# Quad attention of a hybrid encoder: sums by a column of ones, copies on ScalarE, spread loads and weight splits at the end of a turn

## The chip, the core and the metric

One core of a Trainium2 chip runs the whole program. The metric is the device time of the program in microseconds. Engines: TensorE (PE, with its weight loads PEld), VectorE (DVE), ScalarE (ACT), GpSimd (POOL) and SyncE (SP), which here only issues DMAs.

## What is computed

Two sequences of 256 and 512 tokens with 2048 features (768 tokens, six tiles of 128) go through two layers. Each layer is

```python
h = rms_norm(x, ln_g[l]).astype(x.dtype)
proj = jnp.einsum('bsd,de->bse', h, w_in[l])        # q, k, v, gate of mixers A, B, C
ya = window_sink_attention(...)                      # +-128 tokens, bias, sink
yb = global_axial_attention(...)                     # dense, rotary
yc = dilated_mixture_attention(...)                  # three groups of (window, dilation)
mix = concat([ya * silu(ga), yb * silu(gb), yc * silu(gc)])
x = x + jnp.einsum('bse,ed->bsd', mix, w_out[l])
```

The change is in mixer C. It has 8 heads in 2 key groups of 4 heads, each for the patterns `(128, 1), (512, 4), (2048, 16)`. For each pattern

```python
s = jnp.einsum('bqhrd,bqkhd->bhrqk', qblk[:, :, g], kg) + biases[g]
s = jnp.where(valid[None, None, None], s, NEG_INF)
lse = jax.nn.logsumexp(s, axis=-1)
p = jnp.exp(s - lse[..., None])
outs.append(jnp.einsum('bhrqk,bqkhd->bqhrd', p, vg))
```

and the three results of a head are summed with the softmax of their `lse` as weights. All is float32.

## The kernel before

A layer has three phases. First the input projection: PE multiplies normed features by slabs of weights, each as a high and a low part; SP loads the weights, ScalarE rounds the high part (`split_hi`, L1818), DVE subtracts to get the low part (`split_lo`, L2099). Heads are normed, turned and stored to DRAM (`heads_t`, `keys_t`, `v_rows`). Then the attention loop of `N_LOOP` turns, with one step for each turn, while PE also works off pieces of the gate projection (`gate_piece`, L1644 to L1646). Last the output projection. In layer 0 the loop begins at 651 us, in layer 1 at 2028 us.

Steps come in units (`ATT_UNITS`), the quads first. A quad unit takes four heads of mixer C with a dilated pattern; there are four of them, of six steps each (one for each tile of tokens): units 0 and 2 are open (dilation 4), units 1 and 3 packed (dilation 16, where the tokens of a tile fall in four classes of 32, and the four heads of a class share one 128x128 block of scores). So turns 0 to 5 and 12 to 17 score open steps, 6 to 11 and 18 to 23 packed ones. Units of mixer A follow from turn 24. An item is what one query tile is loaded for; in quads items and steps are the same.

In turn i of the quads the engines do, in this order:
- PE: scores of step i (L1674 and L1675 open, L1669 packed); gate pieces; transposes of the probabilities of step i-3 (`p_turn`, L1694); product with the values of step i-4 (`pv`, L1734 open, L1715 packed). Scores have two banks, so those of step i wait until step i-2 is `biased`.
- ScalarE: take the packed product of step i-5 (`take_packed`, L1928), weight splits due (`SPLIT_AT`: turns 0, 9, 15, 22, 25), copy of the turned probabilities of step i-3 if the step is odd (`copy_pt`, L1154), exponentials of step i (`exp_step`: open, L1901, four with `accum_out` for the sums; packed, L1894, one).
- DVE: weight splits due, take the open product of step i-5 (`take_part`, L2293), bias and minima of step i (L2225 open; L2179 to L2186 packed), for packed steps the sums of step i-3 (`packed_sums`, L2192), copy of even steps i-3.
- SP, a queue in order, for item `it`: `load_item(it)` (L1309) once step it-4 is scored; then the stores, key, value, bias and part loads that the tables (`PARTS_AT`, `KEYS_AT`, `VALUES_IN_AT`, `BIASES_AT`, ...) put at that item; then gate weights. `load_bias` (L1297) issues four transfers for a quad unit, `load_blocks` (L1273) eight: they place the values of each class in the diagonal blocks of `blocks0` and `blocks1`, which POOL zeroes before (L2597). Before the loop SP loads biases, keys and values of the first two units and stores the last value slab (`store_values`, L1199).

Results of a quad step, with minima and sums, go into a slot of `part_out` and to DRAM (`store_part`, L1378), and come back in `load_parts` when mixer C merges the three patterns in eight merges.

## Time and profile before

| | us |
|---|---|
| median of 3 runs (2768.97 to 2772.97) | 2769.77 |
| the profiled execution | 2773.48 |
| its span, first to last instruction | 2771.7 |
| PE busy | 2728.9 |
| DVE busy | 1614.7 |
| ScalarE busy | 1190.9 |
| POOL busy | 943.0 |
| quad turns of layer 0 (651.06 to 709.08) | 58.02 |
| quad turns of layer 1 (2028.38 to 2083.23) | 54.85 |

Times in the profile count from the first instruction. A busy time is the sum of an engine's instructions without overlap; those of PE are pipelined, so "busy" is not "at its peak". Matmuls at half clock are also busy. "Idle before, releaser" at the end of a row is the time for which an engine did nothing before that instruction, and what let it go on. SPq is SP's queue of DMA issues: the time there is that of the issue, not of the transfer.

### The profile page before, as it was taken

How to read it: one execution, taken by the hardware profiler on the slowest of the kernel's cores; microseconds unless marked ns; L12 is line 12 of the kernel's file. 1: busy time of each engine (PE TensorE's matmuls, PEld its weight loads, DVE VectorE, ACT ScalarE, POOL GpSimd, SP SyncE). 2: the span in 40 equal slices, each digit the busy share in tenths (PEclk: the TensorE clock that was granted, in tenths of full speed). 3: DMA queues.
4: the chain of work that ended last, by engine and by line, in shares of the span. 5: the costliest groups of instructions: out<-in, count | busy, mean ns of one | idle time of the engine just before them, and what ended most of it. 6: DMA issues, size and time to landing. Idle time of an engine off the chain costs nothing. (4 is left out here: it accounts for less than half of the span.)

```text
span 2771.7 us, 43372 instructions
## 1 busy us (share of the span) xinstructions
PE 2728.9 (98%) x14505; PEld 2444.1 (88%) x14505; DVE 1614.7 (58%) x3901; ACT 1190.9 (43%) x2897; POOL 943.0 (34%) x864
## 2 busy tenths in 40 slices
PE   8999999999999999999999999999999999999999
PEld 7888899988999999988888888999889999998887
DVE  3345644434676677667743466444356766766776
ACT  4322222224565566544542222222256655664443
POOL 0333333320465377600003334333205743774000
PEclk9999999999999999999999999999999999999999
DMA  5366556658544443464524565666685345325535
GB/s 175 105 185 199 181 184 189 180 171 229 149 134 125 118 116 87 145 245 124 202 92 119 187 194 179 193 175 178 184 232 147 115 118 155 94 70 210 198 122 182
DMA packets 439415, 442.53 MB, mean 160 GB/s; under 512 B 103863, under 2 KB 333399, under 8 KB 439196
## 3 DMA queue, kind: packets, MB, share of 16 engines
q1 hardware_dynamic: 439196, 439.77, 53.0%
q8 instruction: 118, 1.93, 0.3%
q14 instruction: 101, 0.83, 0.1%
HBM read 313.91 MB, written 125.75 MB: 159 GB/s over the span
## 5 line engine op out<-in xcount | busy, mean ns | idle before, releaser
L1818 ACT CAST w_hi<-w_raw 128x512 fp32r<-128x512 f32 x640 | 397.2, 622 | 695.2 <-PE bank L1590 430.3
L1588 PE MATMUL bank<-w_hi,act_hi 128*128 128x512 f32 x1728 | 689.1, 399 | 0.0
L2099 DVE TENSOR_TENSOR w_lo<-w_raw,w_hi 128x512 fp32r<-128x512 f32 x640 | 457.8, 716 | 391.9 <-ACT w_hi L1818 389.0
L1590 PE MATMUL bank<-w_hi,act_lo 128*128 128x512 f32 x1728 | 679.0, 393 | 0.0
L1589 PE MATMUL bank<-w_lo,act_hi 128*128 128x512 f32 x1728 | 677.6, 392 | 0.0
L2548 POOL TENSOR_SCALAR prob<-prob,denom 128x256 f32<-128x256 f32 (+2 forms) x288 | 348.8, 1216 | 243.1 <-DVE denom L2263 239.8
L1590 PEld LDWEIGHTS bank<-w_hi,act_lo 128*128 128x128 f32 x1728 | 372.6, 216 | 54.0
L1588 PEld LDWEIGHTS bank<-w_hi,act_hi 128*128 128x128 f32 x1728 | 373.3, 216 | 50.0
L1589 PEld LDWEIGHTS bank<-w_lo,act_hi 128*128 128x128 f32 x1728 | 373.3, 216 | 48.8
L1644 PE MATMUL bank<-act_hi,w_hi 128*128 128x384 f32 x1024 | 348.8, 341 | 0.0
L1646 PE MATMUL bank<-act_hi,w_lo 128*128 128x384 f32 x1024 | 345.9, 338 | 0.0
L1645 PE MATMUL bank<-act_lo,w_hi 128*128 128x384 f32 x1024 | 345.6, 338 | 0.0
L1621 PE MATMUL bank<-w_hi,a_part 128*128 128x512 f32 x672 | 263.2, 392 | 5.7 <-DVE a_part L2391 3.0
L2254 DVE TENSOR_TENSOR pt_lo<-bank,pt_hi 128x256 fp32r<-128x256 f32 (+2 forms) x288 | 154.2, 535 | 188.3 <-ACT pt_hi L1920 186.2
L1622 PE MATMUL bank<-w_lo,a_part 128*128 128x512 f32 x672 | 261.7, 389 | 0.0
L1623 PE MATMUL bank<-w_hi,a_part 128*128 128x512 f32 x672 | 261.6, 389 | 0.0
L2539 POOL TENSOR_TENSOR y<-y,gains 128x256 f32<-128x256 f32 (+1 forms) x144 | 159.8, 1122 | 265.7 <-DVE y L2132 265.7
L2165 DVE TENSOR_TENSOR turned<-bank,turned 128x512 fp32r<-128x512 f32 (+2 forms) x120 | 64.8, 557 | 278.3 <-ACT turned L1885 278.2
L1885 ACT CAST turned<-bank 128x512 fp32r<-128x512 f32 (+2 forms) x120 | 55.3, 482 | 365.0 <-PE bank L1566 355.9
L1694 PE MATMUL bank<-ident,prob 128*128 128x128 f32 x1128 | 195.7, 274 | 5.7 <-POOL prob L2548 5.7
L1645 PEld LDWEIGHTS bank<-act_lo,w_hi 128*128 128x128 f32 x1024 | 193.9, 189 | 4.2
L1914 ACT ACTIVATE prob<-prob,minus_max 128x257 f32<-128x257 f32 (+2 forms) x240 | 128.2, 534 | 161.2 <-DVE minus_max L2245 160.4
(135 smaller groups left out, 4500.7 us busy)
## 6 DMA issues: line engine op xcount, KB each, us to landing
w_raw<-w_in SPq DMA_DIRECT2D x144, 512.0 KB, 4.8
w_sums<-sum_out SPq DMA_DIRECT2D x32, 1280.0 KB, 6.8
w_raw<-w_sums SPq DMA_DIRECT2D x80, 512.0 KB, 4.1
sum_in<-w_out SPq DMA_DIRECT2D x64, 512.0 KB, 5.6
heads_t<-turned SPq DMA_DIRECT2D x240, 128.0 KB, 2.4
q_t<-heads_t SPq DMA_DIRECT2D x192, 128.0 KB, 2.1
k_t<-keys_t SPq DMA_DIRECT2D x48, 384.0 KB, 5.8
w_raw<-w_out SPq DMA_DIRECT2D x32, 512.0 KB, 3.7
```

The lines of the kernel that those rows point to most:

```text
L1588: pe.matmul(acc[t][:], hi, w_hi[:, W_AT[n]:W_AT[n] + SLAB], start=(k == 0), stop=False)
L1589: pe.matmul(acc[t][:], hi, w_lo[:, W_AT[n]:W_AT[n] + SLAB], start=False, stop=False)
L1590: last = pe.matmul(acc[t][:], lo, w_hi[:, W_AT[n]:W_AT[n] + SLAB], start=False, stop=(k == KC - 1))
L1621: pe.matmul(bank[at][:], hi[:, tokens], w_hi[:, W_AT[n]:W_AT[n] + SLAB], start=(j == 0), stop=False)
L1622: pe.matmul(bank[at][:], hi[:, tokens], w_lo[:, W_AT[n]:W_AT[n] + SLAB], start=False, stop=False)
L1623: last = pe.matmul(bank[at][:], lo[:, tokens], w_hi[:, W_AT[n]:W_AT[n] + SLAB], start=False, stop=(j == KH - 1))
L1644: pe.matmul(out, hi, act_hi[:, k, tokens], start=(k == 0), stop=False)
L1645: pe.matmul(out, hi, act_lo[:, k, tokens], start=False, stop=False)
L1646: last = pe.matmul(out, lo, act_hi[:, k, tokens], start=False, stop=(k == KC - 1))
L1818: nc.scalar.copy(w_hi[:, W_AT[n]:W_AT[n] + SLAB], w_raw[:, load % W_RAW, j, :]).then_inc(w_hi_done, 1)
L2099: nc.vector.tensor_tensor(w_lo[:, W_AT[n]:W_AT[n] + SLAB], w_raw[:, load % W_RAW, j, :], w_hi[:, W_AT[n]:W_AT[n] + SLAB].bitcast(F32), ALU ...
L2548: nc.gpsimd.tensor_scalar(v, v, denom[:, pair % STAT_SLOTS, st["r"]:st["r"] + 1], None, ALU.mult)\
```

## The change

- Values get a 65th column of ones: `v_t` and `blocks` are 65 wide, POOL sets the ones, and the quad products write 4 x 65 columns, so that the sum of the probabilities comes out of the product. The exponentials of open steps lose `accum_out`, and `packed_sums` goes, with the waits on it.
- `part_out`, `part_rows` and `part_in` hold, for each head, 64 values, sum and minimum (`ROW` = 66). `load_parts` loses one small transfer.
- `on_act`: ScalarE copies the turned probabilities of all packed steps, and of odd open ones as before.
- `load_blocks` is issued in four pairs, one for each class at successive items (4 to 7 for unit 1, 20 to 23 for unit 3), in place of eight at once (before the loop, and at item 21).
- Biases of quad units 2 and 3 are loaded head by head, at items 11 to 14 and 17 to 20, in place of all four at items 10 and 16.
- Before the loop the last value slab is stored ahead of the loads of keys and biases of unit 1.
- In quad turns other than 0, `split_hi` comes behind the exponentials and `split_lo` behind the copy.

```diff
--- before.py
+++ after.py
@@ -410,7 +409,7 @@
-    return step % 2 == 1
+    return step % 2 == 1 or packed(STEPS[step]["unit"])
...
@@ -630,9 +629,12 @@
 KEYS_AT = at_items((u, UNIT_LAST[u - KV_SLOTS] + 1) for u in range(KV_SLOTS, len(ATT_UNITS)))
-VALUES_IN_AT = at_items((u, UNIT_LAST[u - KV_SLOTS] + PAIR_LAG + 1) for u in range(KV_SLOTS, len(ATT_UNITS)))
+VALUES_IN_AT = at_items((u, UNIT_LAST[u - KV_SLOTS] + PAIR_LAG + 1) for u in range(KV_SLOTS, len(ATT_UNITS)) if not packed(ATT_UNITS[u]))
+BLOCKS_AT = at_items(((u, c), (UNIT_LAST[u - KV_SLOTS] + PAIR_LAG if u >= KV_SLOTS else 0) + c)
+                     for u, x in enumerate(ATT_UNITS) if packed(x) for c in range(CLASSES))
 MERGE_IN_AT = at_items((mc, end - 2 * TT + 1 + PAIR_LAG + 1 if mc == 0 else MERGE_END[mc - 1] + OWN_TURN + 2) for mc, end in enumerate(MERGE_END))
-BIASES_AT = at_items((b, BIAS_LAST[b - 2] + 1) for b in range(2, len(BIAS_SETS)))
+BIASES_AT = at_items(((b, heads), BIAS_LAST[b - 2] + 1 + (1 + heads[0] if BIAS_SETS[b][1] is None else 0))
+                     for b in range(2, len(BIAS_SETS)) for heads in (((0,), (1,), (2,), (3,)) if BIAS_SETS[b][1] is None else ((0, 1),)))
...
@@ -711,7 +713,9 @@
         top[0] -= 4 * TT * 2 * DH
-        blocks1 = sb("blocks1", [P, TT // 2, CLASSES, DH])
+        blocks1 = sb("blocks1", [P, TT // 2, CLASSES, DH + 1])
+        top[0] -= 4 * (TT // 2) * CLASSES * (DH + 1)
+        top[0] += 4 * TT * 2 * DH
...
@@ -1261,18 +1255,18 @@
-            def load_blocks(l, u):
+            def load_blocks(l, u, c):
                 unit = ATT_UNITS[u]
-                sp.wait_ge(blocks_zeroed, 2 * (l + 1))
+                sp.wait_ge(ones_set, 2 * CLASSES * (l + 1))
                 if u >= KV_SLOTS:
...
                 rows = v_rows[:, unit["v"] * DH:(unit["v"] + 1) * DH].rearrange("(h t m c) n -> h c m t n", h=2, t=TT // 2, c=CLASSES)
-                for half, c in itertools.product(range(2), range(CLASSES)):
-                    sp.dma_start(blocks[half][c * PACK:(c + 1) * PACK, :, c, :], rows[half, c]).then_inc(blocks_loaded, 16)
-
-            def load_bias(l, b):
+                for half in range(2):
+                    sp.dma_start(blocks[half][c * PACK:(c + 1) * PACK, :, c, 0:DH], rows[half, c]).then_inc(blocks_loaded, 16)
+
+            def load_bias(l, b, heads=range(4)):
...
@@ -1280,7 +1274,7 @@
                 w = TABLE_COLS[kind]
-                for h in range(4 if hp is None else 2):
+                for h in heads if hp is None else range(2):
...
@@ -1320,13 +1314,12 @@
                 j, hp = first["unit"]["j"], first["hp"]
-                src = part_rows[:, j, hp, :].rearrange("(t p) n -> p t n", p=P)
-                sp.dma_start(part_stat1[:], src[:, :, 2 * DH:PART]).then_inc(part_loaded, 16)
                 for lo, hi in SEQ_TILES:
...
                         rows = part_classes[j, lo + e, 2 * r + hp].rearrange("(t p) n -> p t n", t=hi - lo)
-                        sp.dma_start(class_rows[e:P:hi - lo, lo:hi, r, :], rows).then_inc(part_loaded, 16)
-                sp.dma_start(part_in1[:], src[:, :, 0:2 * DH]).then_inc(part_loaded, 16)
+                        sp.dma_start(part_in0[e:P:hi - lo, lo:hi, r, :], rows).then_inc(part_loaded, 16)
+                sp.dma_start(part_in1.rearrange("p t r n -> p t (r n)"),
+                             part_rows[:, j, 2 * hp:2 * hp + 2, :].rearrange("(t p) r n -> p t (r n)", p=P)).then_inc(part_loaded, 16)
...
@@ -1370,11 +1363,10 @@
                 if packed(unit):
-                    sp.wait_ge(packed_summed, l * N_PACKED + item["packed_no"] + 1)
                     dst = part_classes[unit["j"], item["t"]].rearrange("h (m c) n -> (h m) (c n)", c=CLASSES)
                 else:
-                    row = KV_C * 2 * PART
-                    dst = bass.AP(part_rows.tensor, first * row + unit["j"] * 2 * PART, [[step * row, P], [1, 2 * PART]])
+                    row = KV_C * 4 * ROW
+                    dst = bass.AP(part_rows.tensor, first * row + unit["j"] * 4 * ROW, [[step * row, P], [1, 4 * ROW]])
...
@@ -1457,11 +1449,10 @@
                 load_values(l, 0)
+                for t in range(TT):
+                    store_values(l, NS_IN - 1, t)
                 load_keys(l, 1)
                 load_bias(l, 1)
-                load_values(l, 1)
-                for t in range(TT):
-                    store_values(l, NS_IN - 1, t)
...
@@ -1471,8 +1462,10 @@
                         load_values(l, u)
-                    for b in BIASES_AT.get(it, ()):
-                        load_bias(l, b)
+                    for u, c in BLOCKS_AT.get(it, ()):
+                        load_blocks(l, u, c)
+                    for b, heads in BIASES_AT.get(it, ()):
+                        load_bias(l, b, heads)
...
@@ -1709,10 +1702,11 @@
                         quad_taken(pe, l, q - 2)
+                pe.wait_ge(ones_set, 2 * CLASSES * (l + 1))
                 if packed(st["unit"]):
...
                     half, at = divmod(st["t"], TT // 2)
-                    pe.matmul(o[:, 0:CLASSES * DH], prob_t[:, n % PT_SLOTS, 0:P],
+                    pe.matmul(o[:, 0:CLASSES * (DH + 1)], prob_t[:, n % PT_SLOTS, 0:P],
...
@@ -1721,17 +1715,17 @@
                     if st["kind"] == "Q":
-                        head, kt, first, end = j, st["a"], True, True
-                        tile = values[:, kt, :]
+                        out, first, end = o[:, j * (DH + 1):(j + 1) * (DH + 1)], True, True
+                        tile = values[:, st["a"], :]
                     else:
-                        head, first, end = st["r"], j == 0, j == st["tiles"] - 1
+                        out, first, end = o[:, st["r"] * DH:(st["r"] + 1) * DH], j == 0, j == st["tiles"] - 1
                         at = st["first"] + j * P
...
                         else:
-                            tile = values[:, at // P, :]
-                    last = pe.matmul(o[:, head * DH:(head + 1) * DH], prob_t[:, n % PT_SLOTS, j * P:(j + 1) * P],
+                            tile = values[:, at // P, 0:DH]
+                    last = pe.matmul(out, prob_t[:, n % PT_SLOTS, j * P:(j + 1) * P],
...
@@ -1897,9 +1891,7 @@
                         v = prob[:, n % P_SLOTS, h * P:(h + 1) * P]
-                        at = 2 * DH + h % 2
-                        ins = nc.scalar.activation(v, v, ACT.Exp, bias=part_out[:, q, h // 2, at:at + 1], scale=-1.0,
-                                                   accum_out=part_out[:, q, h // 2, at + 2:at + 3])
+                        ins = nc.scalar.activation(v, v, ACT.Exp, bias=part_out[:, q, h, MIN_AT:MIN_AT + 1], scale=-1.0)
...
@@ -1925,8 +1917,9 @@
                 act.wait_ge(pv_done, l * N_STEPS + item["step"] + 1)
-                nc.scalar.copy(packed_part((l * N_QUADS + item["quad_no"]) % PART_SLOTS)[:, :, 0:DH],
-                               o_bank[item["quad_no"] % 2][:, 0:CLASSES * DH].rearrange("p (c n) -> p c n", n=DH)).then_inc(packed_taken, 1)
+                nc.scalar.copy(part_out[:, (l * N_QUADS + item["quad_no"]) % PART_SLOTS, :, 0:DH + 1],
+                               o_bank[item["quad_no"] % 2][:, 0:CLASSES * (DH + 1)].rearrange("p (c n) -> p c n", n=DH + 1))\
+                    .then_inc(packed_taken, 1)
...
@@ -2039,8 +2032,9 @@
                         fold_pair(l, i - FOLD_LAG)
-                    for c in SPLIT_AT.get(i, ()):
-                        split_hi(l, CHUNKS_IN + c)
+                    if i == 0 or not quads:
+                        for c in SPLIT_AT.get(i, ()):
+                            split_hi(l, CHUNKS_IN + c)
...
@@ -2049,6 +2043,9 @@
                         exp_step(l, i)
+                    if quads and i > 0:
+                        for c in SPLIT_AT.get(i, ()):
+                            split_hi(l, CHUNKS_IN + c)
...
@@ -2185,13 +2182,6 @@
-            def packed_sums(l, i):
-
-                item = ITEMS[STEPS[i]["item"]]
-                dve.wait_ge(exped, l * N_STEPS + i + 1)
-                nc.vector.tensor_reduce(packed_part((l * N_QUADS + item["quad_no"]) % PART_SLOTS)[:, :, DH + 1], class_columns(l, i),
-                                        AX_X, ALU.add).then_inc(packed_summed, 1)
-
...
@@ -2201,8 +2191,6 @@
                     dve.wait_ge(p_turned, n - P_SLOTS + 1)
-                    if packed(STEPS[i - P_SLOTS]["unit"]):
-                        dve.wait_ge(packed_summed, l * N_PACKED + ITEMS[STEPS[i - P_SLOTS]["item"]]["packed_no"] + 1)
...
@@ -2438,7 +2426,7 @@
                     quads = i < QUAD_TURNS
-                    if quads:
+                    if i == 0:
...
@@ -2453,9 +2441,10 @@
                     if quads and i >= T_LAG:
-                        if packed(STEPS[i - T_LAG]["unit"]):
-                            packed_sums(l, i - T_LAG)
                         pt_copy(l, i - T_LAG)
+                    if quads and i > 0:
+                        for c in SPLIT_AT.get(i, ()):
+                            split_lo(l, CHUNKS_IN + c)
...
@@ -2593,8 +2582,13 @@
                 heads_in_dram(pool, l)
+                nc.gpsimd.memset(v_t[:, :, :, DH:DH + 1], 1.0)
                 for values in blocks:
-                    nc.gpsimd.memset(values[:], 0.0).then_inc(blocks_zeroed, 1)
+                    nc.gpsimd.memset(values[:], 0.0).then_inc(blocks_cleared, 1)
+                pool.wait_ge(blocks_cleared, 2 * (l + 1))
+                for values, c in itertools.product(blocks, range(CLASSES)):
+                    nc.gpsimd.memset(values[c * PACK:(c + 1) * PACK, :, c, DH:DH + 1], 1.0).then_inc(ones_set, 1)
+                pool.wait_ge(ones_set, 2 * CLASSES * (l + 1))
...
```

## Rows read from the trace of the kernel before

**Rows 1.** Page, part 1, busy time of each engine over the span

```profile
PE 2728.9 (98%) x14505; PEld 2444.1 (88%) x14505; DVE 1614.7 (58%) x3901; ACT 1190.9 (43%) x2897; POOL 943.0 (34%) x864
```

**Rows 2.** Windows; columns: from:to, us, busy us (count) of each engine, granted clock, DMA share, GB/s

```profile
651.06:709.08 58.02, 51.89 (x357) 48.22 (x356) 37.53 (x176) 30.03 (x128) 2.01 (x2) 0.89 0.83 233
675.00:687.00 12.00, 11.86 (x53) 10.75 (x53) 5.83 (x37) 7.77 (x34) 0.00 (x0) 0.57 0.87 229
705.00:714.00 9.00, 7.61 (x28) 7.06 (x29) 3.68 (x15) 2.80 (x9) 0.00 (x0) 0.62 0.51 162
696.00:699.00 3.00, 3.00 (x29) 2.97 (x26) 2.75 (x8) 0.63 (x2) 0.00 (x0) 1.00 0.60 149
...
2028.38:2083.23 54.85, 47.95 (x356) 44.68 (x356) 37.02 (x174) 29.41 (x127) 2.00 (x2) 0.96 0.86 246
2064.00:2070.00 6.00, 6.00 (x40) 5.90 (x39) 3.68 (x20) 4.43 (x21) 0.00 (x0) 0.72 0.76 226
2079.00:2086.00 7.00, 4.81 (x20) 4.49 (x21) 3.67 (x15) 1.15 (x5) 0.00 (x0) 0.76 0.75 241
```

**Rows 3.** Waits, 650 to 715: who waited for whom, us in total, times, longest

```profile
PE bank L1669 <- DMA quad_t<-heads_t: 4.6, 2, 3.3
...
PE bank L1734 <- DVE prob_t L1154: 0.6, 1, 0.6
```

**Rows 4.** Waits, 2027 to 2090, columns as in rows 3

```profile
PE bank L1669 <- DMA quad_t<-heads_t: 3.1, 2, 2.6
...
PE bank L1734 <- DVE prob_t L1154: 2.3, 1, 2.3
...
PE bank L1715 <- DVE prob_t L1154: 0.8, 1, 0.8
```

**Rows 5.** Time line of SP's queue; columns: start, us, engine, line, what

```profile
665.32 2.12 SPq L1297 DMA_DIRECT2D bias<-bias_rows  x4
...
667.49 0.47 SPq L1309 DMA_DIRECT2D quad_t<-heads_t  x1
...
692.66 3.71 SPq L1273 DMA_DIRECT2D blocks<-v_rows  x8
...
698.50 2.10 SPq L1297 DMA_DIRECT2D bias<-bias_rows  x2
...
700.65 0.43 SPq L1309 DMA_DIRECT2D quad_t<-heads_t  x1
```

**Rows 6.** Time line of PE in layer 0, idle time before in brackets

```profile
673.75 0.63 PE L1669 MATMUL bank<-k_t,quad_t 128*128 128x64 f32 x4 [1.25 <-DMA quad_t<-heads_t]
...
692.94 0.61 PE L1669 MATMUL bank<-k_t,quad_t 128*128 128x64 f32 x4
...
696.08 0.97 PEld L1734 LDWEIGHTS bank<-v_t,prob_t 128*128 128x128 f32 x8
```

**Rows 7.** Time line around turns 15 and 16 of layer 1

```profile
2061.03 0.69 DVE L2099 TENSOR_TENSOR w_lo<-w_raw,w_hi 128x512 fp32r<-128x512 f32 x1 [3.06 <-ACT w_hi L1818]
...
2063.23 1.10 PE L1734 MATMUL bank<-v_t,prob_t 128*128 128x64 f32 x8 [2.27 <-DVE prob_t L1154]
```

**Rows 8.** Groups by form, whole span: line, engine, what, count, busy us, mean ns, idle before

```profile
L1901 ACT ACTIVATE prob<-prob,part_out 128x128 f32<-128x128 f32 x96 | 37.2, 392 | 16.2 <-DVE part_out L2225 16.2
...
L1901 ACT ACTIVATION_READ_ACCUMULATOR prob<-prob,part_out 128x1 f32 x96 | 18.2, 190 | 0.0
...
L1154 DVE COPY prob_t<-bank 128x128 f32<-128x128 f32 x12 | 3.4, 282 | 0.0
...
L1894 ACT ACTIVATE prob<-prob 128x128 f32<-128x128 f32 x24 | 7.5, 310 | 35.0 <-DVE prob L2186 35.0
...
L2192 DVE TENSOR_REDUCE part_out<-prob 128x4 f32<-128x128 f32 x24 | 6.8, 282 | 0.0
...
L1154 ACT COPY prob_t<-bank 128x128 f32<-128x128 f32 x12 | 3.2, 267 | 6.3 <-PE bank L1694 6.1
```

49 lines of the change are left out of this document (20 added, 29 removed).

## Prediction

> **What bounds the kernel now.** I read the busy times first: TensorE (PE) is busy for 98% of the span [rows 1], so nearly everything runs at its pace, and only places where PE idles or runs slowly can give time back. The windows show where that is: the two quad stages, one for each layer. In them PE idles for 58.02 - 51.89 = 6.1 us in layer 0 and for 54.85 - 47.95 = 6.9 us in layer 1, and its granted clock means 0.89 and 0.96 [rows 2]. Four stretches in or just behind the two stages run in part at half clock (1.2 GHz in place of 2.4): 12 us at 0.57, 9 us at 0.62, 6 us at 0.72 and 7 us at 0.76. Against full clock they lose 12 x 0.43 = 5.2, 9 x 0.38 = 3.4, 6 x 0.28 = 1.7 and 7 x 0.24 = 1.7 us [rows 2]. Each follows a stall of PE. DMA is busy for 0.83 and 0.86 of the stages, thus 48.2 and 47.2 us [rows 2]: a second limit, close behind PE.
>
> The waits of PE name the stalls: query tiles, 4.6 and 3.1 us; the DVE copy of turned probabilities before an open value product, 0.6 and 2.3 us; the same copy before a packed one, 0.8 us in layer 1 [rows 3, 4]. Time lines give the causes. I number turns from 0 in each layer, with one turn per step: 0-5 and 12-17 open, 6-11 and 18-23 packed.
> - Turn 11 (stall A): SP stood in four bias issues for 2.12 us and only then asked for the query tile, at 667.49; PE idled 1.25 us for it until 673.75 [rows 5, 6]. In layer 1 the same wait is what remains of 3.1 when the longest is taken off, 0.5 us [rows 4].
> - Turn 23 (stall C): SP spent 3.71 us on eight block issues, then went through a query tile, a store, keys and two biases, and asked for the last tile at 700.65 [rows 5]; PE waited 3.3 us for it, and 2.6 in layer 1 [rows 3, 4].
> - Turns 15-16 (stall B, layer 1): DVE has its weight split first in the turn and stood 3.06 us until ScalarE, behind with its exponentials, had done its half. The minima and the copy came behind it, and PE idled 2.27 us before the product of turn 16 [rows 7].
>
> **The change part by part.** The sum is made against the profiled execution, 2773.48 us with a span of 2771.7; it lies 3.7 above the median 2769.77, so I take the sum off the median.
>
> *Bias loads of quad units, one head for each item.* The same bytes and instructions go out, later. For the third unit one issue (0.53) stands behind each of the items 11 to 14, in place of four (2.12) ahead of item 11, so that tile is asked for about 2 us sooner and with 512 KB less in front. That covers 1.25 and 0.5 us: 1.7. The half-clock stretch 675-687 hangs on stall A: layer 1 has a 0.5 us stall at the same place, and its mean of 0.96 (54.85 x 0.04 = 2.2 us lost) is used up by the stretches behind stalls B and C, so nothing fell there [rows 2]. I take its 5.2 us in full. Bounds 0 and 5.2; I choose the top because the two layers differ in little else there.
>
> *Ones beside the values, ScalarE copies all packed steps.* An exponential with its accumulator is busy for 392 ns, with the accumulator's read of 190 ns partly under it [rows 8]. Without the read it costs between 392 - 190 = 202 and 392 ns; I take 300, near the 310 ns of the packed exponential, which has no accumulator [rows 8]. An open step then asks 1.2 in place of 1.57 us of ScalarE. It also gets the DVE half of the packed copies, 267 ns each [rows 8], and stays below two microseconds in turns that last 54.85 / 24 = 2.3 on the mean. DVE loses the packed sums and half of the packed copies, 282 ns each [rows 8]. On PE the 65th column widens products that are paced by weight loads of 0.11 us (0.97 for 8, [rows 6]); packed ones grow by 4 in 256 columns, some 7 ns a step. Both are nil. The new memsets (eight of one column, one for the values) lie on POOL ahead of the stage, where it is busy for 2 of 58 us and less [rows 2]; their readers come at the first products: nil.
>
> *Splits last in a turn.* Minima and copy no longer stand behind the split. Both parts together remove stall B: 2.3 + 1.7 (clock) in layer 1, 0.6 in layer 0, and 0.8 of the packed product's wait: 5.4, of which I take 5. The new position has a price. The split of turn 15 on DVE now waits for ScalarE's exponentials of turn 15 itself (about 1.2 us) and for its split, and the minima of turn 16 are queued behind it; PE has two score banks and copies are wanted one turn later, so most is covered. I charge 0.5 a layer, bounds 0 and 3.1, DVE's idle time before its split in rows 7.
>
> *Block loads in four pairs.* For the last unit two issues (3.71 / 4 = 0.93 us) stand behind each of items 20 to 23. Turn 18 is scored from 692.94 to 693.4 [rows 6]; from there to the request for tile 23 SP has item 22, a store and keys (2.1, as from 696.37 to 698.50), one pair of blocks 0.93 and biases 2.1: 5.1 us, so a request near 698.5 in place of 700.65 [rows 5]. Of 3.3 and 2.6 us I take 2.0 and 1.5: 3.5. The half-clock losses behind it (3.4 + 1.7) I leave, as a stall remains; bounds 0 and 5.1. What is late next is the last pair of blocks itself: it is issued behind tile 23 and the packed product of turn 22 wants all eight.
>
> *Order at the start.* Keys of the second unit (768 KB) and its biases move behind the value stores, close to the stage's start, and its blocks into items 4 to 7. Two block issues and the load of gate weights now stand before item 5, whose tile has the least lead. I charge 1.0 a layer, bounds 0 and 2.
>
> *Last bias head.* Head 3 of the third unit is issued behind item 14 (turn 10 scored) and DVE wants it in turn 12; PE meets that wait two turns later. I charge 0.5 a layer, bounds 0 and 3, the upper one a stall like C.
>
> *Merge loads.* One transfer of 16-byte pieces less for each of eight merges, the rest alike: PE does not wait for merges in any row of these stages; 0.
>
> Sum: 1.7 + 5.2 + 5 + 3.5 - 2 x (0.5 + 1.0 + 0.5) = 11.4 us less. 2769.8 - 11.4 = 2758.4; I say 2759.
>
> The rows for the half clock have it behind each of the larger stalls [rows 2 to 4]. The Trainium skill, page "TensorE: Matmul & The Clock Gate", section "HAM oscillation", says that long gaps while waiting for DMA make the clock fall, and that the half rate is then paid on top of the gap. By it the 5.2 us go with stall A, and if every gap goes, all four stretches do: that is the second rival. The trace agrees in that no stretch stands without a stall ahead of it.
>
> The row for bias loads is that the tile issued behind them was used 6.3 us later, 667.49 to 673.75 [rows 5, 6]. The Trainium skill, page "DMA: Bandwidth & Descriptors", section "Queues, rings and completion order", says that each DMA engine takes descriptors in ring order; spreading then moves the burst behind another tile and doesn't shrink it. This speaks against the change and is the first rival.
>
> **The rivals.** *Transfers are the bound.* The stages need 48.2 and 47.2 us of DMA, and at the start 768 KB of keys come closer to each. So the stages stay above some 50 and 49 us; at most 8 + 6 are saved in them, and 3 to 4 of half clock behind them. If DMA keeps its present share of 0.85, stalls A and C come back at other turns with their clock, and only stall B is saved, 2.3 + 1.7 + 0.6 = 4.6 us: 2765. For it: a share of 0.83 and 0.86 over the whole stages. Against: it falls to 0.60 at 696-699, behind SP's block issues [rows 2].
>
> *The clock stays up.* Stall C shrinks enough that nothing falls: 5.1 more and half of the charges back, 2752. Against it: SP still issues 5 us of work there.
>
> *Slower: the last bias head is late.* It lies behind tile 14 and a store, and DVE waits for all four in turn 12, with its copies and the weight splits queued behind. PE meets the wait when it scores turn 14, four turns after the issue: 4 x 2.3 less some 2 us for the two issues ahead of it and DVE's minima, about 7 us. The tile of 667.49 took 6.3 [rows 5, 6]. Were it 11 us, PE would stall for 4 in both layers, in the turns where layer 0 lost 5.2 us to the clock: (4 + 5.2) x 2 = 18.4, so 7 slower than before: 2777. It outweighs the 11.4 from 5.7 us a layer on, thus from a landing after 7.5 us if the clock falls with it.
>
> **Chances.** Forecast (2755 to 2764) 0.55; clock stays up 0.15; transfers bound 0.19; slower 0.11. A measurement of this kernel tells 0.2% (5.5 us) from no change. Faster 0.70, same 0.19, slower 0.11. The range 2751 to 2769 leaves out the slower case and the tail of the fast one.
>
> **What would show it.** Windows of 12 us from turn 12 at clock 1.0 (stall A right); no idle before the product of turn 16; exponentials at a pitch near 0.30; PE's wait for query tiles at about 3 in place of 7.7 us; stages of about 51 us in both layers. Wrong if PE waits for blocks or for DVE held by a bias load, or if half-clock stretches turn up at new turns.

## The result, and where the time went

The changed kernel is slower. Median 2786.17 us over 8 executions beside 2773.49 for the kernel before; the ratio is 1.0049 (95% interval 1.0027 to 1.0071). Run again later it gave 1.0042 (1.0028 to 1.0056). The forecast was 2759 and faster.

The time of either kernel moves by 18 to 20 us between executions, together with the mean granted clock of TensorE. A straight line through 124 executions of the kernel before gives 2773.3 us at a clock of 0.995 and 1.94 us less for each 0.001 more; the executions scatter about it by 1.5 us. Two more executions of that kernel, at clocks of 0.85 and 0.87, took 2983 and 5179 us and are left out everywhere. Below, "at an equal clock" means the mean distance from this line (plus or minus two standard errors). The changed kernel lies at +11.4 (±0.7) over 20 executions, with a mean clock of 0.9943 (±0.0012) where the kernel before has 0.9947 (±0.0003). So the clock explains next to nothing of the difference: 0.0004 by this line is 0.8 us, within the error.

### The profile page after: what moved, and what is told of

It reads as the page before. It is cut to its first block and busy times, and to the rows that moved or that the text cites. A ratio compares the mean times of both kernels' runs of the same rounds, so it can differ in the third digit from the quotient of the medians.

```text
span 2792.8 us, 43314 instructions
## 1 busy us (share of the span) xinstructions
PE 2753.4 (99%) x14505; PEld 2457.5 (88%) x14505; DVE 1607.7 (58%) x3865; ACT 1184.8 (42%) x2813; POOL 946.0 (34%) x882
## 5 line engine op out<-in xcount | busy, mean ns | idle before, releaser
L1614 PE MATMUL bank<-w_hi,a_part 128*128 128x512 f32 x672 | 268.6, 400 | 3.4 <-DVE a_part L2379 2.5
L1616 PE MATMUL bank<-w_hi,a_part 128*128 128x512 f32 x672 | 265.3, 395 | 0.0
L1637 PEld LDWEIGHTS bank<-act_hi,w_hi 128*128 128x128 f32 x1024 | 194.5, 190 | 4.1
```

The source lines that it names most:

```text
L1614: pe.matmul(bank[at][:], hi[:, tokens], w_hi[:, W_AT[n]:W_AT[n] + SLAB], start=(j == 0), stop=False)
L1616: last = pe.matmul(bank[at][:], lo[:, tokens], w_hi[:, W_AT[n]:W_AT[n] + SLAB], start=False, stop=(j == KH - 1))
L1637: pe.matmul(out, hi, act_hi[:, k, tokens], start=(k == 0), stop=False)
```

## The profile after

The profiled execution took 2796.29 us (span 2792.8, clock 0.990): it is the slowest of its 20. First its windows: the two quad stages, then the two half-clock stretches in layer 1. Columns as in [rows 2].

```profile
649.87:704.70 54.83, 47.29 (x357) 44.13 (x356) 35.04 (x166) 26.80 (x85) 2.01 (x2) 0.97 0.90 257
2028.85:2099.59 70.74, 66.62 (x356) 64.03 (x356) 36.13 (x166) 26.63 (x86) 2.00 (x2) 0.67 0.74 199
...
2042.00:2063.00 21.00, 21.00 (x91) 20.10 (x90) 9.67 (x29) 4.25 (x14) 0.00 (x0) 0.51 0.68 171
2073.00:2101.00 28.00, 28.00 (x119) 27.04 (x120) 13.61 (x51) 6.94 (x22) 0.00 (x0) 0.51 0.63 181
```

The stage of layer 0 is 3.2 us shorter than in [rows 2], the one of layer 1 is 15.9 longer, and the clock accounts for more than all of that: 70.74 x 0.33 = 23.3 us lost, where the kernel before lost 2.2. The second profile of the same kernel, with 2777.7 us of span and a clock of 0.997, shows how little of this belongs to the change:

```profile
649.92:706.26 56.34, 47.31 (x356) 44.11 (x355) 35.24 (x166) 26.86 (x85) 2.00 (x2) 0.95 0.90 249
2029.58:2083.70 54.12, 46.87 (x356) 44.07 (x356) 34.86 (x166) 26.63 (x85) 1.99 (x2) 0.96 0.91 261
```

Here the stages take 56.3 and 54.1 us, beside 58.0 and 54.9 before: 2.4 us less in sum. What does not move between the two profiles is the output projection. Its three groups of matmuls, first of the kernel before, then of the changed one; the last two numbers ahead of the idle time are busy us and mean ns:

```profile
L1621 PE MATMUL bank<-w_hi,a_part 128*128 128x512 f32 x672 | 263.2, 392 | 5.7 <-DVE a_part L2391 3.0 <-DVE x_cols L2404 2.0 <-DVE x_cols L2406 0.7
...
L1622 PE MATMUL bank<-w_lo,a_part 128*128 128x512 f32 x672 | 261.7, 389 | 0.0
L1623 PE MATMUL bank<-w_hi,a_part 128*128 128x512 f32 x672 | 261.6, 389 | 0.0
```

```profile
L1614 PE MATMUL bank<-w_hi,a_part 128*128 128x512 f32 x672 | 268.6, 400 | 3.4 <-DVE a_part L2379 2.5
L1616 PE MATMUL bank<-w_hi,a_part 128*128 128x512 f32 x672 | 265.3, 395 | 0.0
L1615 PE MATMUL bank<-w_lo,a_part 128*128 128x512 f32 x672 | 263.9, 393 | 0.0
```

No line of this code was edited, and yet these matmuls, 1008 in a layer, take 4 to 8 ns more on the mean. From the first to the last of them a layer needs 241.1 and 238.4 us where it needed 236.0 and 233.2: 10.3 us in all, at a granted clock of 1.000. This is the term that the prediction did not have. What changed for these matmuls is an address: `v_t` grew by 48 bytes and `part_in1` by 96, and as the kernel rounds each start up to a multiple of 32, everything laid out behind them in SBUF (the on-chip memory) moved by 160 bytes. `a_part`, whose tiles they hold as weights, went from byte 214848 to 215008; `w_hi` and `w_lo`, which they stream, stayed where they were. The input projection's weights, `act_hi` and `act_lo`, did not move (`ROW_START` puts them 320 bytes past a multiple of 512 in both kernels), and its three groups of 1728 matmuls show 399, 393 and 392 ns in both.

The waits of PE in layer 0 of the first profile, the answer to [rows 3]:

```profile
PE bank L1709 <- DMA blocks<-v_rows: 4.1, 1, 4.1
PE bank L1667 <- DVE part_out L2213: 1.6, 2, 1.4
PE bank L1662 <- DMA quad_t<-heads_t: 0.6, 1, 0.6
PE bank L1667 <- DMA quad_t<-heads_t: 0.6, 1, 0.6
PE bank L1728 <- DVE prob_t L1151: 0.4, 1, 0.4
```

The tiles of turns 11 and 23 are in time. The copy of turned probabilities costs 0.4 us here, where it had cost 0.6 [rows 3], and nothing in layer 1, where it had cost 2.3 [rows 4]. In their place stand 4.1 us for the blocks in turn 22, 1.4 behind DVE's minima in turn 14, and tiles in turns 5 and 6. The times of issue and use:

```profile
671.97 0.43 SPq L1291 DMA_DIRECT2D bias<-bias_rows  x1
...
694.34 0.89 SPq L1267 DMA_DIRECT2D blocks<-v_rows  x2
```

```profile
676.07 0.29 DVE L2213 CUSTOM_DVE_ANT_0 prob<-bank,bias 128x128 f32<-128x128 f32 x1 [2.15 <-DMA bias<-bias_rows]
```

```profile
701.17 1.21 PE L1709 MATMUL bank<-blocks,prob_t 128*128 128x260 f32 x2 [4.13 <-DMA blocks<-v_rows]
```

The last bias head is asked for at 671.97 and DVE stands until 676.07; the last pair of blocks is asked for at 694.34 and PE stands until 701.17. ScalarE's part of the change did what was expected:

```profile
651.87 3.62 ACT L1894 ACTIVATE prob<-prob,part_out 128x128 f32<-128x128 f32 x12 [5.46 <-DVE part_out L2213]
```

Twelve exponentials in 3.62 us, a pitch of 0.30. The exponentials of this line still last 392 ns each on the mean in this profile, so they overlap.

## Experiments

"Idle" is the time of a quad stage less PE's busy time in it, in one profile; where much of a stage ran at half clock PE is busy for longer and the idle time comes out smaller (4.1 us at a clock of 0.67), so stages at different clocks are not compared closely. OP is the output projection, first to last matmul, in layers 0 and 1.

| kernel | ratio to before (95%) | at equal clock, us | idle, layers 0 + 1 | OP, us |
|---|---|---|---|---|
| before | 1 | 0 | 6.1 + 6.9 | 236.0, 233.2 |
| changed, both runs | 1.0049, 1.0042 | +11.4 ±0.7 | 7.5 + 4.1; 9.0 + 7.3 | 241.1, 238.4 |
| e1_align | 1.0042 (1.0027 to 1.0058) | +11.0 ±1.5 | | 240.4, 237.8 |
| e2_shift32 | 1.0028 (1.0017 to 1.0039) | +9.9 ±0.8 | | 241.0, 238.4 |
| e2_shift64 | 1.0031 (1.0018 to 1.0045) | +10.0 ±1.0 | | 241.0, 238.4 |
| e6_op320 | 0.9995 (0.9984 to 1.0005) | +1.0 ±0.9 | 7.4 + 7.9 | 236.0, 233.2 |
| e4_loads | 1.0002 (0.9986 to 1.0018) | +1.8 ±1.0 | 7.0 + 5.1 | 235.9, 233.2 |
| e3_compute | 1.0036 (1.0019 to 1.0054) | +7.7 ±1.7 | | 240.2, 237.7 |
| e12_compute320 | 0.9996 (0.9982 to 1.0011) | -2.4 ±1.0 | 6.4 + 3.8 | 235.9, 233.1 |
| e8_blocks1 | 0.9987 (0.9973 to 1.0000) | -0.7 ±0.6 | | 235.9, 233.2 |
| e7_retimed | 0.9980 (0.9968 to 0.9991) | -2.7 ±1.3 | | 235.9, 233.2 |
| e11_start | 0.9979 (0.9968 to 0.9990) | -2.3 ±1.2 | 7.9 + 6.6 | 235.9, 233.2 |
| e9_best | 0.9981 (0.9966 to 0.9997) | -5.2 ±0.6 | 5.8 + 5.7 | 235.9, 233.3 |
| e10_fewbytes | 0.9974 (0.9964 to 0.9984) | -4.9 ±0.6 | 5.6 + 6.0 | 236.0, 233.2 |
| e13_gatelater | 0.9960 (0.9944 to 0.9975) | -6.2 ±1.1 | 2.9 + 5.0 | 235.9, 233.1 |

**Is it the address? Four runs.** First a shift of `a_part` within the kernel before, with nothing else edited:

```
+        top[0] += 32          # e2_shift32; 64 in e2_shift64
         gate_t = sb("gate_t", [P, GATE_SLOTS, TOKENS])
```

> The kernel before with one edit: 32 bytes are left free ahead of gate_t, so that gate_t, the bias tables and a_part start 32 bytes past a multiple of 64. prob, prob_t and quad_t stay where they are. Theory address: the output projection alone slows, its matmuls from 392 to about 400 ns and its two stretches from 239 and 238 to 244 and 243 us, so the kernel is about 10 us slower than before (ratio 1.0036), with the rest unchanged. If the gate, the bias tables or the clock were what slows the matmuls in the changed kernel, or if alignment is nothing, the ratio is 1.000 within 0.001. Rival that address costs more elsewhere (bias tables read by VectorE): the quad stages grow by over 1 us each.

```profile
L1622 PE MATMUL bank<-w_hi,a_part 128*128 128x512 f32 x672 | 267.1, 397 | 3.5 <-DVE a_part L2392 2.6
L1624 PE MATMUL bank<-w_hi,a_part 128*128 128x512 f32 x672 | 265.8, 396 | 0.0
L1623 PE MATMUL bank<-w_lo,a_part 128*128 128x512 f32 x672 | 265.8, 395 | 0.0
```

These are its groups by form: 5 to 7 ns more a matmul, from 32 bytes. Both output projections slow by 5.0 and 5.2 us, and the kernel by 9.9 at an equal clock. The address alone does it, and it is that of `a_part`, the only one of the tensors moved here that these matmuls read; the input projection keeps its 399, 393 and 392 ns. The rule that I had in mind, multiples of 64, was tested with the next two.

```
-P_COLS = 4 * P + 4
+P_COLS = 4 * P + 2            # e1_align, on the changed kernel
```

> The changed kernel with each of the four slots of prob two columns narrower (514 instead of 516; 513 are used), so that everything laid out behind prob in SBUF moves down by 32 bytes: the partial activations a_part of the output projection, the transposed probabilities and quad_t start at a multiple of 64 bytes again, as in the kernel before, instead of 32 bytes past one. Nothing else differs. Theory address: the output projection's matmuls are slower in the changed kernel (first line 399.7 ns instead of 391.9) because of where their operand lies; they return to about 392 ns, the two output projections from 244.3 and 243.2 us to 239 and 238, and the time falls by about 10 us against the changed kernel at an equal granted clock, to 2765 to 2778. Rival: the slower matmuls come from the granted clock (0.990 in the profiled run against 0.996) or another cause that lies in the attention; then they stay at 395 to 400 ns and the time at 2778 to 2796. Neither theory says that the half-clock stretches in the quad stage of layer 1 (70.8 us) go; if they are set off by the idle times at turns 5, 6 and 17 they stay, at 60 to 71 us for this stage.

It missed: `a_part` at 214976 is a multiple of 64, and the output projections stay at 240.4 and 237.8.

> The kernel before with 64 bytes, instead of 32, left free ahead of gate_t: a_part starts at 214912, a multiple of 128 bytes (384 past a multiple of 512). Theory place: the place modulo 512 counts and 320 is the good one: the two output projections take 240 to 241 and 238 us as with the shift of 32 bytes, their matmuls 395 to 400 ns, kernel about 8 to 10 us slower than before at an equal clock. Rival: a multiple of 64 bytes is enough; then 236 and 233 us and no difference to the kernel before. The run with a_part at 214976 already speaks against the rival, but there the rest of the kernel was the changed one.

At 214912, a multiple of 128, it is no better. What is left is the very place. The fourth run brings it back in the changed kernel:

```
-P_COLS = 4 * P + 4
+P_COLS = 4 * P + 2
...
-        top[0] = max(top[0], heads_from)
+        top[0] = max(top[0], heads_from - 128)
```

> The changed kernel with its loads as they are, and with the address of a_part (and of gate_t, the bias tables, the transposed probabilities and quad_t) brought back to the very bytes of the kernel before: 32 bytes come from narrower slots of prob and 128 from an earlier start of q_t, k_t and v_t. a_part then starts at byte 214848, 320 bytes past a multiple of 512, where the run with 214976 (448 past) and the kernel before with 214880 (352 past) took 240 to 241 and 238 us for the two output projections. Theory place: the remainder by 512 counts, not the one by 64, so the two output projections return to 236 and 233 us, their matmuls to 392, 389 and 389 ns, and the kernel is about 10 us shorter than the changed one at an equal granted clock: 2770 to 2785. Rival: the slower output projection comes with something else of the change than this address, and stays at 240 and 238 us. The quad stages keep their idle times and half-clock stretches (55 to 71 us each).

```profile
L1614 PE MATMUL bank<-w_hi,a_part 128*128 128x512 f32 x672 | 263.3, 392 | 5.7 <-DVE a_part L2379 2.9 <-DVE x_cols L2392 2.0 <-DVE x_cols L2394 0.7
L1616 PE MATMUL bank<-w_hi,a_part 128*128 128x512 f32 x672 | 261.6, 389 | 0.0
L1615 PE MATMUL bank<-w_lo,a_part 128*128 128x512 f32 x672 | 261.6, 389 | 0.0
```

The groups by form are those of the kernel before to the nanosecond. The changed kernel falls from +11.4 to +1.0 at an equal clock: 10.4 us, the 10.3 of the output projections. That is shown for this kernel at five places: 320 bytes past a multiple of 512 is fast, 352, 384, 448 and 480 past are not. That the remainder by 512 is what counts, and not another property of byte 214848, was not tried, and what in the engine costs the 5 ns is not shown. Nor do moved weights slow every matmul: those of 64 columns that hold `prob_t` as weights show a mean of 266 ns in e6_op320 and in the changed kernel, where `prob_t` lies 160 bytes further on.

**Which half of the change does what? Three runs.** The loads alone, on the kernel before (with the changed start order and `load_blocks` and `load_bias` for one class and one head at a time):

```
+BLOCKS_AT = at_items(((u, c), (UNIT_LAST[u - KV_SLOTS] + PAIR_LAG if u >= KV_SLOTS else 0) + c)
...
+BIASES_AT = at_items(((b, heads), BIAS_LAST[b - 2] + 1 + (1 + heads[0] if BIAS_SETS[b][1] is None else 0))
```

> The kernel before with the new order of loads alone: blocks in pairs over items and biases one head an item, the last values stored ahead of the keys and bias of unit 1. Columns, copies, splits and addresses stay as in the kernel before. Theory loads: the idle before turns 5 and 6 and the late last pair of blocks, which in the changed kernel precede the half clock of layer 1 and the fall at 699 us in layer 0, come with the new order, so here the quad stage of layer 1 rises from 54.9 to 60 to 71 us, while the stall of turn 11 is gone and the one of turns 15 and 16 stays; the time is 2767 to 2785. Rival compute: the half clock comes with the work that was taken from the engines in the packed turns and the later splits; then both stages here are at 52 to 56 us and the time at 2762 to 2768.

The loads theory holds in its waits: 2773.43 us, stages of 55.9 and 63.6 us, and waits for tiles in turns 5 and 6 (1.0 and 0.7 us; 0.8 and 0.5 in layer 1) and for blocks (2.1). The 63.6 us have 27 us at half clock in them, behind the old stall of turn 16; e12_compute320, with the loads of the kernel before, has 24 us of it in its layer 1, so this is a draw and no proof. At an equal clock the new order of loads costs 1.8 us; it gains nothing.

The rest of the change with the loads of the kernel before, at the slow and then at the fast address:

```
-BIASES_AT = at_items(((b, heads), BIAS_LAST[b - 2] + 1 + (1 + heads[0] if BIAS_SETS[b][1] is None else 0))
+BIASES_AT = at_items(((b, heads), BIAS_LAST[b - 2] + 1)
...
                 load_keys(l, 1)
                 load_bias(l, 1)
+                for c in range(CLASSES):
+                    load_blocks(l, 1, c)
```

> The changed kernel with the aligned addresses (prob slots of 514 columns) and with the loads in the order of the kernel before: unit 1's keys, bias and blocks ahead of the last stores of values, all blocks of a unit at once, all heads of a bias at once. What is left of the change is the column of ones, ScalarE's share of the copies and the splits at the end of a turn. Theory loads: the stall at turn 11 is back (4 to 5 us with its half clock in one or both layers), the one of turns 15 and 16 stays away, there is no half clock from turn 6 on in layer 1, both quad stages take 50 to 57 us and the time is 2762 to 2770. Rival compute: layer 1's quad stage takes over 62 us here as well, and the time is over 2772.

> The part of the change that is not loads, now with the addresses of the kernel before: columns of ones, ScalarE's copies and the splits at the end of a turn, while all loads of keys, bias, blocks and tiles are issued as in the kernel before. The same kernel with a_part at 214976 was 7.7 us over the kernel before at an equal granted clock, of which the output projections took 8.7. Theory sum: the output projections return to 236 and 233 us, and what is left is the stall of turns 15 and 16 that this part removes: 1 to 3 us less than the kernel before at an equal clock (ratio 0.999), with the loads part alone at 1.5 us more and the whole change at the old addresses at 1.0 more. Rival: the split of the parts does not add up, and this one is 4 us or more under the kernel before; then the new order of loads costs that much and hides it.

2783.2 us at the slow address is on the rival's side, but the stage of layer 1 takes 53.2 us, where the rival wanted over 62: what both had left out was the output projection. At the fast address it comes to -2.4. The stall of turns 15 and 16 is gone, yet only part of its price came back. The waits of PE in e12_compute320, layer 0 and layer 1:

```profile
PE bank L1664 <- DMA quad_t<-heads_t: 6.1, 2, 4.1
```

```profile
PE bank L1669 <- DMA quad_t<-heads_t: 2.5, 2, 1.7
PE bank L1664 <- DMA quad_t<-heads_t: 1.0, 1, 1.0
```

PE is ahead of where it was, and now waits 9.6 us for tiles where it had waited 4.6 + 3.1 [rows 3, 4]. The two halves sum to -2.4 + 1.8 = -0.6, beside +1.0 ±0.9 for the whole at the old addresses: they add up within their errors.

**What holds the tiles and the blocks? Six runs**, all with the addresses of e6_op320. Unit 1's blocks two items later:

```
-BLOCKS_AT = at_items(((u, c), (UNIT_LAST[u - KV_SLOTS] + PAIR_LAG if u >= KV_SLOTS else 0) + c)
+BLOCKS_AT = at_items(((u, c), (UNIT_LAST[u - KV_SLOTS] + PAIR_LAG if u >= KV_SLOTS else 2) + c)
```

> The run before this one (addresses as in the kernel before) with one edit more: the four pairs of block loads of unit 1 go to items 6 to 9 instead of items 4 to 7, so that no pair stands ahead of the tiles of turns 5 and 6 in SP's queue. Theory queue: the idle times of 0.6 to 1.7 us before turns 5 and 6, which wait for quad_t, go in both layers; with them goes the half clock that in layer 1 begins at 2040 to 2042 us. The later idle times (about 1.5 us at turn 14 for the last bias head, 2.5 to 4.3 us at turn 22 for the last pair of blocks) stay, each with its half clock. Quad stages 53 to 58 us, kernel 2766 to 2776. Rival: the idle time comes back as a wait of the product of turn 10 for the blocks of unit 1 (issued up to turn 5 or 6, landing in 4 to 7 us), or the half clock comes without an idle time of over 1 us before it; then the stage stays at 58 us or more.

The time is in the range, but the reason is not: idle times of 0.9 and 0.5 us in layer 0 and 1.7 in layer 1 remain before turns 5 and 6. The pairs of blocks were not what held these tiles. At an equal clock the run is even so 1.7 us (give or take 1.1) under e6_op320, and where that comes from is not shown.

Then unit 3's blocks and the bias heads earlier as well:

```
-BLOCKS_AT = at_items(((u, c), (UNIT_LAST[u - KV_SLOTS] + PAIR_LAG if u >= KV_SLOTS else 2) + c)
+BLOCKS_AT = at_items(((u, c), UNIT_LAST[u - KV_SLOTS] + PAIR_LAG + c // 2 if u >= KV_SLOTS else 2 + c)
...
-BIASES_AT = at_items(((b, heads), BIAS_LAST[b - 2] + 1 + (1 + heads[0] if BIAS_SETS[b][1] is None else 0))
+BIASES_AT = at_items(((b, heads), BIAS_LAST[b - 2] + 1 + (heads[0] if BIAS_SETS[b][1] is None else 0))
```

> As the run before, and two edits more: the last two pairs of blocks of unit 3 are issued one and two items earlier (two pairs an item at items 19 and 20, not one pair at each of 19 to 22), and the four bias heads of unit 2 and their like at one item earlier (from item 10). Theory landings: the idle time at turn 22 (waiting for blocks) and at turns 12 to 14 (waiting for the last bias head) both vanish, and with them the half-clock stretches that follow them; quad stages 50 to 53 us in both layers, granted clock 0.998 or more, kernel 2757 to 2766, under the kernel before. Rival queue: four block loads at one item hold SP for 1.7 us and a tile comes late instead, with an idle time of over 1 us and a half clock at turns 19 to 23; then a stage takes 55 us or more and the kernel 2766 to 2775.

The wait for blocks is gone in both layers, -2.7 at an equal clock, and as the rival said a tile comes late instead: 3.9 us at turn 23 of layer 1. The start order next:

```
                 load_values(l, 0)
-                for t in range(TT):
-                    store_values(l, NS_IN - 1, t)
                 load_keys(l, 1)
                 load_bias(l, 1)
+                for c in range(CLASSES):
+                    load_blocks(l, 1, c)
+                for t in range(TT):
+                    store_values(l, NS_IN - 1, t)
```

> The changed kernel with the addresses of the kernel before (a_part at byte 214848) and one edit to its loads: the order ahead of the loop is that of the kernel before, with unit 1's keys, bias and all its blocks ahead of the last six stores of values. Unit 3's blocks and the bias heads stay spread. Theory bytes: the changed start order puts keys, bias and blocks of unit 1 (2.2 MB more inside the quad stage: 14.3 against 12.1 MB, DMA share 0.92 against 0.80) beside the tiles of turns 5 and 6, and that is why these come late. With the old order the idle times before turns 5 and 6 fall from 0.7 to 1.9 us each to under 0.8 together, the stage begins about 1 us later, and the last bias head and the last pair of blocks find more room: their idle times at turns 14 and 22 shrink or stay. Quad stages 52 to 56 us, kernel 2764 to 2772, 3 to 5 us less than the same kernel with the new start order at an equal clock. Rival: it is the number of instructions in SP's queue and not the bytes; then the gain is under 1 us, as moving the block pairs alone gave.

The idle times before turns 5 and 6 fall to 1.1 us together in layer 0 and 0.4 in layer 1. The step from +1.0 to -2.3 is 3.3 us (give or take 1.5), so the new start order, with unit 1's blocks spread over items 4 to 7, costs 1.7 a layer; e8_blocks1 leaves open how much of it is the blocks. The last bias head did not profit: PE idles 2.2 us for it in layer 0 and 1.3 in layer 1. The figure of 2.2 MB in this expectation was mine and wrong: it took one window of equal length in both kernels, and in the kernel before the stage was not over by then. To the same boundaries, start to end of the stage, it is 58.02 us at 233 GB/s, 13.5 MB, before [rows 2], and 54.83 at 257, 14.1 MB, after. e9_best is e11_start with the ends of both spread loads earlier; the lines are against the changed kernel:

```
-BLOCKS_AT = at_items(((u, c), (UNIT_LAST[u - KV_SLOTS] + PAIR_LAG if u >= KV_SLOTS else 0) + c)
+BLOCKS_AT = at_items(((u, c), UNIT_LAST[u - KV_SLOTS] + PAIR_LAG - 1 + (c + 1) // 2)
...
-BIASES_AT = at_items(((b, heads), BIAS_LAST[b - 2] + 1 + (1 + heads[0] if BIAS_SETS[b][1] is None else 0))
+BIASES_AT = at_items(((b, heads), BIAS_LAST[b - 2] + 1 + (heads[0] if BIAS_SETS[b][1] is None else 0))
```

> As the run before, and the tails of both spread loads earlier: unit 3's pairs of blocks at items 19, 20, 20, 21 (instead of 20 to 23), bias heads from item 10 (instead of 11). Theory landings: the idle time at turn 22 for blocks falls from about 4 us to under 1, the one at turn 14 for the last bias head goes, and no tile comes late by over 1 us, as fewer bytes are inside the stage. Quad stages 50 to 53 us, kernel 2758 to 2765, the fastest of all here. Rival: with four block loads at one item the tile of turn 22 or 23 is late by 1 to 4 us as in the kernel before; then 2764 to 2770.

```profile
648.64:700.08 51.44, 45.69 (x356) 42.92 (x356) 33.52 (x161) 25.30 (x82) 2.00 (x2) 0.99 0.89 261
2018.63:2070.75 52.12, 46.39 (x357) 43.83 (x356) 33.37 (x162) 26.09 (x84) 2.02 (x2) 0.98 0.90 260
```

These are its two stages, 6.6 and 2.7 us shorter than in [rows 2]; at an equal clock 5.2 of these 9.3 us stand. There is no wait for blocks, but one for the tile of turn 23, 2.5 and 3.2 us, as the rival had it and against the expectation of under 1. Then fewer bytes, on e6_op320. This kernel leaves out most of the weights of the first gate pieces, so its output is not that of the layer and only its timing counts:

```
+GATE_CUT = 24
...
-                    sp.dma_start(w_raw[:, n % W_RAW, :, :].rearrange("p j (k n) -> p (j k) n", n=P), gate_weights(l, m))\
+                    few = 8 if m * PER_LOAD < CHUNKS_IN + GATE_CUT else P
+                    sp.dma_start(w_raw[:, n % W_RAW, :, :].rearrange("p j (k n) -> p (j k) n", n=P)[:, :, 0:few], gate_weights(l, m)[:, :, 0:few])\
```

> The changed kernel with the addresses of the kernel before, and the weight loads of the first gate pieces cut to 8 of 128 columns, so that three loads of 512 KB in the quad stage (items 4, 5 and 20) move 32 KB each: 1.4 of 14.3 MB taken away. The gate's first tiles are computed from stale weights; all else is as it was. Order and number of issues are unchanged. Theory bytes: tiles and blocks land late because the 16 queues of transfers are full (DMA share 0.92 to 1.0), so with less to move the idle times before turns 5 and 6 fall by over half and the one at turn 22 (behind the load of item 20) from about 4 to under 3 us; DMA share falls. Rival: the time of issue sets the landing; then the idle times stay as they are with full loads (0.7 and 1.7, 4 us).

```profile
PE bank L1711 <- DMA blocks<-v_rows: 3.8, 1, 3.8
PE bank L1669 <- DVE part_out L2215: 1.7, 2, 1.5
PE bank L1669 <- DVE prob L2185: 0.2, 1, 0.2
```

The waits of layer 0; layer 1 has the first two at 3.7 and 2.2. No wait for a tile is left in turns 5 and 6: there the bytes in front were the cause. The waits for the last pair of blocks (3.8 and 3.7, where e6_op320 has 4.2 and 3.8) and for the last bias head hardly moved; e7_retimed, which issues both earlier, has neither, so there the time of issue is what counts. Each theory holds at its own turns. Last, the same weights loaded in full but behind the stage, on e9_best:

```
+GATE_LATER = {W_RAW + 1: 21, W_RAW + 2: 23}
-GATE_LOADS_AT = at_items((m, SPLIT_TURN[PER_LOAD * (m - W_RAW) + PER_LOAD - 1] + 1 if PER_LOAD * (m - W_RAW) + PER_LOAD - 1 >= LEAD else 0)
+GATE_LOADS_AT = at_items((m, max(GATE_LATER.get(m, 0), SPLIT_TURN[PER_LOAD * (m - W_RAW) + PER_LOAD - 1] + 1 if PER_LOAD * (m - W_RAW) + PER_LOAD - 1 >= LEAD else 0))
```

> The fastest kernel so far (addresses and start order of the kernel before, unit 3's blocks at items 19, 20, 20 and 21, bias heads from item 10) with one edit: two loads of gate weights of 512 KB each, issued at items 5 and 20 though their columns are needed from turns 33 and 37, move to items 25 and 27, behind the quad stage. Theory bytes: 1.0 of 13.5 MB leave the stage, the tile of turn 5 comes in time and the tile of turn 22 waits less than 2.5 and 3.2 us; the stages fall from 51.4 and 52.1 to 49 to 51 us and the kernel by 1 to 4 us at an equal clock, to 2758 to 2764. Rival issue: what holds the tile of turn 22 is the order of SP's queue (keys of 768 KB and two biases just ahead of it); then its wait stays at 2.5 to 3.2 us and only turn 5 gains, under 1 us a layer. Third: the two loads come too late where they went and the attention behind the stage grows.

```profile
PE bank L1670 <- DMA quad_t<-heads_t: 1.0, 1, 1.0
PE bank L1665 <- DMA quad_t<-heads_t: 0.9, 2, 0.7
...
PE bank L1665 <- DMA quad_t<-heads_t: 3.4, 1, 3.4
```

The first two lines are waits of layer 0, the last one of layer 1. The wait that the expectation puts at turn 22 is that of turn 23's tile: it fell from 2.5 to 0.7 us in layer 0 and stayed in layer 1 (3.2, 3.4). Whether bytes or order hold it there stays open. At an equal clock the step from -5.2 to -6.2 is within its error. The version is faster than both kernels, by 0.40% (0.25 to 0.56) than the kernel before, with a median of 2761.06 us.

**Is the low clock the change's doing?** The changed kernel once more, unedited.

> The changed kernel again, as it is, for two numbers of which there are only eight executions: its granted clock and its time at an equal clock. Theory place plus transfers: at an equal granted clock it is 10 to 12 us over the kernel before (10.3 from the two output projections, 1 from the quad stages), and its mean clock is that of the kernel before within 0.001 (0.9947 over 104 executions), so that the 70.8 us of the first profile's quad stage in layer 1 is one draw among many; a second profile shows the two quad stages at other lengths, with their sum between 108 and 126 us. Rival: the change makes long stretches at half clock more likely by itself; then the mean clock is 0.993 or less again and a quad stage of over 65 us comes again in layer 1.

No sign of it: mean clock 0.9946 in these twelve, at +11.4 for an equal clock, and stages of 56.3 and 54.1 us. The 70.7 us stage of the first profile was one draw; over all 20 executions the mean clock is known to 0.0012, or 2.3 us by the line.

## Why the prediction was wrong

The sum was 11.4 us less; measured at an equal clock it is 11.4 more. (The median of three executions that the sum started from, 2769.8, lies 3.7 under that of eight, which is part of the 27 us between 2759 and 2786 and no step of the mechanism.) Two things failed: the sum priced nothing outside the quad stages, where 10.3 us were lost, and inside them it took removed stalls as saved, where the waits moved to the next late transfer. By its steps:

- **"Both are nil."** Wide of the mark for what the wider columns move, not for the columns. A packed product of 260 columns has a median of 384 ns beside 381 for 256 columns: nil within 3 ns, as said. But the 48 bytes in `v_t` and 96 in `part_in1` moved `a_part`, and that cost 10.3 us in a phase that the diff does not touch. The working went through instructions and waits and never asked which addresses change. This is the largest single error. Without it the kernel comes out the same as before (+1.0, e6_op320) and not slower; the 12.4 us between that and the forecast lie in the steps that follow.
- **Stall A (1.7).** Right: the tile of turn 11 comes in time.
- **Its half-clock stretch (5.2, taken in full).** Wrong in kind. A stretch at half clock was read as the property of a stall, out of one execution. Over the executions the mean clock does not differ (0.9943 and 0.9947), while single profiles have stages with 0.5 us (e9_best, layer 0) to 23.3 us lost to it. The term should have been 0 with a spread.
- **Stall B (5).** The mechanism was right: pitch of 0.30, no idle above 0.4 us before the product of turn 16. The size was half: the whole compute part gives 2.4 us (give or take 1.0). In its one profile PE then waits for tiles, 9.6 us where it had been 7.7, which would account for most of the rest.
- **Stall C (3.5).** The prediction named what is late next, the last pair of blocks, and charged nothing for it. That wait is 4.1 us in one stage of the first profile and 4.1 in both of the second (4.2 and 3.8 in e6_op320), more than the 3.3 and 2.6 that it replaced [rows 3, 4].
- **Last bias head (0.5 a layer, bounds 0 and 3).** PE idles 1.4 us for it in layer 0 of the first profile and 1.5 and 1.4 us in the second: three times the charge, within its bounds. The landing took 676.07 - 671.97 = 4.1 us. The slower rival had this mechanism and needed 7.5 us; it was not what made the kernel slower.
- **Start order (1.0 a layer, bounds 0 and 2).** 1.7 a layer, with unit 1's blocks as in the prediction, and within its bounds.

Together: the quad stages give +1.0 ±0.9 in place of -11.4, and the output projections +10.3 in place of 0. The rival "transfers are the bound" had the right mechanism for the stages. It said that stalls A and C come back at other turns and that only stall B is saved; idle time in the two stages is 13.0 us before and 16.3 in the second profile of the changed kernel, at a DMA share of 0.90 and 0.91 beside 0.83 and 0.86 [rows 2]. It still kept 4.6 us that were not there. The start order, which put 0.6 MB more into the stage (13.6 MB in e11_start, without it), takes 3.3 of them at an equal clock. The chance of 0.11 for slower was given to one mechanism inside the edited stage; a mechanism outside it had none.

The Trainium skill, page "DMA: Bandwidth & Descriptors", section "Queues, rings and completion order", with descriptors taken in ring order, was on the side of this rival. The trace bears that out at turns 5 and 6, where the waits for tiles went with 1.4 MB of the bytes around them (e10_fewbytes), and not at turn 22, where the wait stayed at 3.7 and 3.8 us.

## What to carry to other kernels

When an edit changes the size of a buffer, list every tensor whose address moves and look at the matmul durations of phases that were not edited; put a padding or a fixed address there before judging the edit. Where transfers fill a stage as they do here (0.83 to 0.91 of it), removing one stall can move the idle time to the next late landing, so cost that landing first, take bytes out of the stage (e11_start, 3.3 us) and issue the late loads earlier (e9_best, another 2.9). Take no half-clock stretch of a single profile into a sum: compare at an equal granted clock, over many executions.

## What the runs showed of the hardware

- Matmuls of 128x512 in float32 took 389 to 392 ns with their weights at byte 214848 of a partition and 393 to 400 ns with them at 214880, 214912, 214976 or 215008, at a granted clock of 1.000. The weight loads themselves show 188 ns in both, so the loss is not visible in the rows of the loads. Matmuls of 128x64 with weights moved by 160 bytes showed 266 ns in both.
- In the quad stages the granted clock fell to half (1.2 GHz) behind idle times of PE, of 0.95 us (e13_gatelater, layer 0) to 4.3 us (e1_align), but not behind each of them: the 1.4 us of turn 14 in layer 1 of the second profile passed without. The length did not follow the idle time: 20 and 27 us behind 1.7 and 1.4 us in layer 1 of the first profile, 3.4 us behind 4.0 in layer 1 of e8_blocks1. The Trainium skill, page "TensorE: Matmul & The Clock Gate", section "HAM oscillation", says that long gaps while waiting for DMA make the clock fall and that the half rate is paid on top; the traces agree with that for gaps of 3 to 4 us. They show besides that it can fall behind gaps of 1 to 2 us, and that what is paid differs by some 12 us (half of 27 - 3.4) and isn't larger for the longer gap.
